# Two pairs of buffers for h's parts, and the first and last gate of each FFN in halves

## The reference

```python
def swiglu(x, w_gate, w_up, w_down):
    return (jax.nn.silu(x @ w_gate) * (x @ w_up)) @ w_down
...
        x = layer_norm(ALPHA * x + FFN_RESIDUAL * swiglu(x, ffn1_w_gate[l], ffn1_w_up[l], ffn1_w_down[l]),
                       ln1_g[l], ln1_b[l])
```

## Time and profile before

| | |
|---|---|
| median of 3 runs | 958.84 us (958.73 to 960.05) |
| the profiled execution's own time | 960.52 us |
| its span, first to last instruction | 958.5 us |
| mean granted TensorE clock | 0.998 |
| TensorE busy | 947.2 us, 99% of the span |
| VectorE busy | 853.7 us, 89% |
| ScalarE busy | 633.1 us, 66% |

### The profile page before, as it was taken

How to read it: one execution, slowest core, us unless ns; L and a number is a source line. 1 busy time by engine, 2 the same in 40 slices (tenths; PEclk the granted TensorE clock), 3 DMA queues, 4 the chain that set the end, 5 groups by cost and what they waited for, 6 DMA issues and landing times.

```text
span 958.5 us, 15322 instructions
## 1 busy us (share of the span) xinstructions
PE 947.2 (99%) x5418; PEld 817.6 (85%) x5418; DVE 853.7 (89%) x1119; ACT 633.1 (66%) x771; POOL 26.7 (3%) x55
## 2 busy tenths in 40 slices
PE   9999999999999999999999999999999999999996
PEld 9978888888788988888998888898888889888885
DVE  6999998966899999998999999988578989999986
ACT  6666665568884667675566767655688765667653
POOL 0000000001101000000000000000010100000000
PEclk9999999999999999999999999999999999999999
DMA  8576645672344565555636484654633445555554
GB/s 318 209 264 229 253 175 178 217 263 89 132 154 159 217 211 212 185 212 185 220 132 220 176 306 175 219 177 177 220 143 119 171 159 202 221 176 220 175 188 154
DMA packets 34653, 187.28 MB, mean 195 GB/s; under 512 B 3888, under 2 KB 3888, under 8 KB 19504
## 3 DMA queue, kind: packets, MB, share of 16 engines
q1 hardware_dynamic: 33120, 177.22, 51.4%
q0 software_dynamic: 1488, 9.45, 2.5%
HBM read 185.61 MB, written 1.05 MB: 195 GB/s over the span
## 4 chain that ended last, share of the span: by engine, by line
PE 91%; DVE 6%; issue 1%; DMA 1%; ACT 0%; DVEq 0%; POOL 0%; SPq 0%; ACTq 0%; POOLq 0%
PE bank L1599 67%; PE bank L1455 8%; PE bank L1457 8%; PE bank L1456 8%; PE bank L1518 1%; DVE w_lo L952 1%; DVE w_lo L909 1%; DMA raw<-stream 1%; DVE stick_t L931 1%; PE bank L1830 1%; DVE h_lo L1143 0%; DVE w_lo L959 0%; DVE stick_t L938 0%; DVE stick_t L941 0%; DVE w_lo L918 0%
## 5 line engine op out<-in xcount | busy, mean ns | idle before, releaser
L1599 PE MATMUL bank<-xT,w_hi 128*128 128x512 f32 (+1 forms) x1248 | 397.2, 387 | 0.0
L1599 PEld LDWEIGHTS bank<-xT,w_lo 128*128 128x128 f32 x1200 | 223.2, 188 | 49.7
L1599 PE MATMUL bank<-xT,w_lo 128*128 128x256 f32 x1200 | 234.6, 278 | 0.0
L510 ACT ACTIVATE w_hi<-raw 128x2048 fp32r<-128x2048 f32 x116 | 221.8, 1912 | 2.0 <-DMA raw<-stream 1.9
L1599 PEld LDWEIGHTS bank<-xT,w_hi 128*128 128x128 f32 x1248 | 198.0, 189 | 6.0 <-issue 0.9
L909 DVE TENSOR_TENSOR w_lo<-raw,w_hi 128x2048 fp32r<-128x2048 f32 x54 | 123.5, 2287 | 10.2 <-ACT w_hi L510 10.0
L651 ACT ACTIVATE ez<-bank 128x512 f32<-128x512 f32 x64 | 38.5, 601 | 104.0 <-PE bank L1599 104.0
L1599 PE MATMUL bank<-w_hi,h_hi 128*128 128x512 f32 x252 | 98.6, 391 | 2.3 <-DVE h_lo L1143 2.3
L1599 PE MATMUL bank<-w_lo,h_hi 128*128 128x512 f32 x252 | 98.6, 391 | 0.0
L1599 PE MATMUL bank<-w_hi,h_lo 128*128 128x512 f32 x252 | 98.4, 391 | 0.0
L1455 PE MATMUL bank<-xT,w_hi 128*128 128x256 f32 x304 | 86.2, 284 | 0.0
(11 more groups left out here) (189 smaller groups left out, 1577.7 us busy)
## 6 DMA issues: line engine op xcount, KB each, us to landing
raw<-stream SPq DMA_DIRECT2D x110, 1024.0 KB, 4.8
raw<-stream SPq DMA_DIRECT2D x110, 512.0 KB, 4.5
lnp<-ln_gb POOLq DMA_DIRECT2D x6, 1024.0 KB, 5.1
band<-rel_band POOLq DMA_DIRECT2D x2, 1024.0 KB, 9.8
xn<-x POOLq DMA_DIRECT2D x1, 1024.0 KB, 6.7
out<-xn SPq DMA_DIRECT2D x4, 256.0 KB, 2.0
qT<-first SPq DMA_DIRECT2D x2, 384.0 KB, 4.1
kT<-first SPq DMA_DIRECT2D x2, 384.0 KB, 5.1
```

Of the source, the lines that this page charges most:

```text
L510: nc.scalar.activation(w_hi[:, at(slot if into is None else into)], raw[:, slot, :], ACT.Copy).then_inc(hi_ready, 1)
L1599: return nc.tensor.matmul(o, w, x, start=start, stop=stop, skip_group_check=True)
```

## The change

Each pair of h_hi and h_lo gets a twin, in space that attention uses (sp_hi, sp_lo). Step j uses pair j mod 2, and so the loops over j on three engines are written with two steps in a body. With two pairs, high_h(j) need not wait for the products of unit j - 1; it moves ahead of copy_gate(j, 0) on ScalarE, and low_h(j) moves ahead of two subtractions on VectorE. gate(1) and gate(SF) become two halves like the other gates, with five matmuls between them; ScalarE copies both halves, and VectorE adds them. In the first FFN up of unit 1 goes to bank 7, not 6. Around the end of an FFN some of VectorE's instructions change places.

```diff
+        H_HI, H_LO = ((h, flat(s)[:, 0:7 * P].rearrange("p (i t) -> p i t", i=7))
+                      for h, s in ((h_hi, sp_hi), (h_lo, sp_lo)))
...
-                def high_h(j):
+                def high_h(j, k):
                     act.wait_ge(hsum_done, seven_step(l, f, j) + 1)
-                    nc.scalar.activation(h_hi[:, :, :], hs[:, 1:8, :], ACT.Copy).then_inc(hhi_done, 1)
+                    nc.scalar.activation(H_HI[k][:, :, :], hs[:, 1:8, :], ACT.Copy).then_inc(hhi_done, 1)
...
-                def last_of_h_and_parts(j):
+                def last_parts(j):
                     act.wait_ge(unit_used, used(l, base + 3 * j + 1))
-                    high_h(j)
                     split_last_parts_hi(l, f, j)
 
-                def step(j, more=True):
+                def step(j, k, more=True):
                     up_hi(j + 1)
+                    high_h(j, k)
+                    copy_gate(j, 0)
                     differences(j)
-                    copy_gate(j, 0)
-                    last_of_h_and_parts(j)
+                    last_parts(j)
                     copy_gate(j, 1)
...
-                differences(1)
-                up_hi(2)
-                last_of_h_and_parts(1)
-                act.wait_ge(hf_done, it(l, f, 1) + 1)
-                silu(2, 5)
-                next_gate(1)
-                copy_up(2, 0)
-                next_pure(2)
-                copy_up(2, 1)
-                with act.Fori(2, SF - 1) as j:
-                    step(j)
-                step(SF - 1, more=False)
+                step(1, 1)
+                with act.Fori(1, (SF - 1) // 2) as i:
+                    for k in range(2):
+                        step(2 * i + k, k)
+                step(SF - 1, 0, more=False)
                 split_hi(l, base + 3 * SF + 3, 0, first[0] + 1 + SF)
+                copy_gate(SF, 0)
...
-                silu(FP - 1, 3 * SF + 2)
+                copy_gate(SF, 1)
                 split_hi(l, base + 3 * SF + 5, 2, first[2] + 1 + SF)
+                silu_sums(SF)
...
-                def low_parts(j):
+                def low_parts(j, k):
                     split_up_lo(l, base + 3 * j + 3, 0)
+                    low_h(j, k)
+                    split_up_lo(l, base + 3 * j + 3, 1)
                     split_differences_lo(l, f, j)
-                    split_up_lo(l, base + 3 * j + 3, 1)
-                    low_h(j)
                     split_last_parts_lo(l, base + 3 * j + 4)
                     gate_sum(j)
...
+                split_lo(l, base + 3 * SF + 3, 0)
                 gather(l, f, 2)
-                split_lo(l, base + 3 * SF + 3, 0)
...
                 gather(l, f, 3)
+                gate_sum(SF)
                 split_lo(l, base + 3 * SF + 4, 1)
                 split_lo(l, base + 3 * SF + 5, 2)
                 last = 2 * l + f == 2 * DEPTH - 1
+                gated(FP - 1, 3 * SF + 3, M[1])
                 if not last:
                     dve.wait_ge(next_first_hi, 2 * l + f + 1)
...
-                gate(1)
-                step(1, first=True)
-                with pe.Fori(2, SF - 1) as j:
-                    step_with_gate(j)
-                step_with_gate(SF - 1, stop=True)
-                rest(stop=True)
-
-                gate(SF)
+                gate_half(1, 0)
+                rest(0, start=True)
+                gate_half(1, 1)
+                step(1, 1)
+                with pe.Fori(1, (SF - 1) // 2) as i:
+                    for k in range(2):
+                        step_with_gate(2 * i + k, k)
+                step_with_gate(SF - 1, 0, stop=True)
+                gate_half(SF, 0)
+                rest(0, stop=True)
+                gate_half(SF, 1)
```

More of the change, by code:

```diff
@@ L611, in ffn @@
                                              ACT.Copy).then_inc((first_hi, hi_ready)[half], 1)
-                    high_h(0)
+                    high_h(0, 0)
                     first_unit_hi()
@@ L1165, in ffn @@
                     split_pure_lo(l, f, 0)
-                    low_h(0)
+                    low_h(0, 0)
                     split_differences_lo(l, f, 0)
@@ L1184, in ffn @@
                     if j == 0 and r < 0:
-                        gated(j + 1, 3 * j + 3, bank[6])
+                        gated(j + 1, 3 * j + 3, bank[7])
                         split_lo(l, base + 3 * j + 5, 2)
@@ L1193, in ffn @@
                     split_pure_lo(l, f, j + 1)
[L1194 to L1203, removed]
                 def gate_sum(j):
@@ L1225, in next_unit @@
                     h_sums(j + 1)
-                split_last_parts_lo(l, base + 7)
+                low_parts(1, 1)
                 next_unit(1)
[L1229 to L1233, removed]
+                with dve.Fori(1, (SF - 1) // 2) as i:
+                    for k in range(2):
+                        low_parts(2 * i + k, k)
+                        next_unit(2 * i + k)
+                low_parts(SF - 1, 0)
                 split_lo(l, base + 3 * SF + 2, 2)
@@ L1253, in ffn @@
                     nc.vector.tensor_tensor(w_lo[:, c], raw[:, 0, HALVES[0]], w_hi[:, c].bitcast(F32), ALU.subtract)
-                gated(FP - 1, 3 * SF + 3, M[1])
+                dve.wait_ge(hhi_done, it(l, f, FP - 1) + 1)
+                nc.vector.tensor_tensor(hl_lo[:, :, :].rearrange("p c (b t) -> p c b t", b=2), h_pair,
+                                        hl_hi[:, :, :].bitcast(F32).rearrange("p c (b t) -> p c b t", b=2),
+                                        ALU.subtract).then_inc(hlo_done, 1)
                 if not last:
@@ L1619, in ffn @@
                 base = FFN_BASE[f]
-                def gate(j):
-                    pe.wait_ge(silu_done, it(l, f, j) + 1)
-                    pe.wait_ge(up_copied, 2 * wide(l, f, j) + 2)
-                    columns(l, base + 3 * j + 2, 2, bank[0])
                 def gate_half(j, c):
@@ L1646, in up_half, with product @@
                     wide_half(bank[0], 0, c).then_inc(unit_used if c else up_first, 1)
-                def product(m, start=False, signal=None, parts=(0, 1, 2)):
+                def product(k, m, start=False, signal=None, parts=(0, 1, 2)):
                     a, b = WINOGRAD[m]
                     w = at(1, seven(b))
-                    h = (h_hi[:, a, :], h_hi[:, a, :], h_lo[:, a, :])
+                    h = (H_HI[k][:, a, :], H_HI[k][:, a, :], H_LO[k][:, a, :])
                     d = (w_hi[:, w], w_lo[:, w], w_hi[:, w])
@@ L1658, in product, with rest, step @@
                         last.then_inc(signal, 1)
-                def rest(stop=False):
-                    product(6, signal=m_done if stop else None, parts=(1, 2))
-                    product(4, signal=unit_used)
-                def step(j, stop=False, first=False):
+                def rest(k, start=False, stop=False):
+                    product(k, 6, signal=m_done if stop else None, parts=(1, 2))
+                    if start:
+                        pe.wait_ge(hf_done, it(l, f, 1) + 1)
+                    product(k, 4, start, unit_used)
+                def step(j, k, stop=False):
                     n = seven_step(l, f, j)
```

67 lines of the change are left out of this document (30 added, 37 removed).

## The result

The change made the kernel slower by a little: median 962.09 us over 11 runs (961.45 to 962.35) against 959.36 of the kernel before (11 runs, 958.62 to 960.05). The ratio is 1.0028, 95% interval 1.0020 to 1.0036. The forecast was 958.2 us with a range to 960.4, so both the sign and the range were wrong. The profiled execution of the change took 962.09 us with a span of 960.3 us, against 960.52 and 958.5 before. So the two traces show 1.8 us of the 2.7 between the medians, since the profiled execution of before lay above its median.

What follows compares the result with a forecast made beforehand. It took TensorE, busy 947.2 of 958.5 us, as the bound. Terms +0.16 + 2 x 0.02 - 0.24 - 0.76 gave -0.80, or -0.54 without the late load; between them, 958.84 - 0.67 = 958.2 us, range 955.6 to 960.4.

Steps and rivals of the forecast that it cites:

- The end of an FFN: Last gate of each FFN: halves save 0.19 us, what follows the gated product is unchanged; 0.76 us in all.
- The gated product's margin: End of the second FFN: VectorE free at 466.71, gated product may start at 466.73, so it just fits, by 0.02 us.
- The waits at the first gates: Before gate_half(j, 1), TensorE waits for ScalarE's copy behind high_h: 0.67 and 1.10 us in the first FFN, 0.11 in the second and third.
- VectorE's delay of 0.40: First FFN, unit 2: gate_sum(1) takes 0.60 where a 0.20 wait stood, so h_sums(2) ends 0.40 us later.
- the 2.86 that the new buffers were to bring: Two waits of TensorE for h_lo, 1.52 and 1.14 us, go, with twice 0.10 of restart.
- three signs of being wrong: h_sums(2) moves by more than 0.4, the gated product starts later than 0.3 after the columns, or span falls over 2 us.
- The late load: Fourth FFN: a weight load landed late, perhaps in that execution alone; without it the sum is -0.54 us, not -0.80.
- Gates in halves: First and last gate of each FFN: two halves take 5.56 us against 5.75, 0.19 less for each of eight gates, 1.52.
- VectorE becomes the bound: Slower rival: eight more sums on VectorE, 4.8 us, all on the path, less 1.52 saved; 962.1 us, 9%.
- The waits just go: Faster rival: the gate's copy isn't held by high_h, gain 4.4 us, 954.5; needs h_sums(2) 1.1 us sooner; 8%.
- The double bodies: Slower rival: two-step loop bodies miss their code at backward branches, 8.5 us where engines overlap, 966.7 us; 3%.

Runs made afterwards that it cites:

- last_whole: The changed kernel with the last gate by columns() and no gate_sum there, VectorE's new order at the end kept; 961.37 us, ratio 1.0021.
- tail_before: The changed kernel with the whole end of an FFN as in the kernel before: last gate by columns(), no sum, VectorE's old order; 959.52 us, ratio 1.0002.
- tail_order: The changed kernel with the first half split back ahead of the gated product and the other ahead of hl_lo, gate still in halves; 962.32 us, ratio 1.0029.
- copy_first: The changed kernel with ScalarE's copy of the gate's first half ahead of high_h in every step; 958.53 us, ratio 0.9991.
- after_again: The changed kernel, unedited, run and profiled a second time; 962.81 us, ratio 1.0028 to the kernel before.
- before_again: The kernel before the change, unedited, run and profiled a second time; 959.72 us, ratio 0.9997.
- after_pad: The changed kernel with 64 unused semaphore increments at the head of TensorE's program, shifting its code; 971.19 us, ratio 1.0123.
- copy_buffers: The changed kernel with the gate's copy ahead of high_h, the old FFN end, and the first gate by columns() too; 957.25 us, ratio 0.9975.
- copy_tail_before: The changed kernel with the gate's copy ahead of high_h and the old FFN end, first gate still in halves; 956.25 us, ratio 0.9966.
- pool_half: The changed kernel with the first half split of the next stage's low weights at an FFN's end given to GpSimd; 962.27 us, ratio 1.0027.

## Why the prediction was wrong

**The end of an FFN is the step that failed.** The prediction said: "What follows is the same in both: one half of a split (1.22) between gated and hl_lo, only another half. So 0.19 in each FFN, 0.76 in all." That counts the instructions between the gated product and hl_lo alone, and there it is right. But the half split that was ahead of the gated product had to go somewhere, and it went behind hl_lo, ahead of the layer norm. The distance from the gated product to the norm's first addition grew by 1.24 us, and TensorE waited 0.64, 0.99 and 0.80. last_whole against tail_before shows that the order alone costs 1.85 us. tail_order shows that putting it back ahead of the gated product doesn't mend it, as long as gate_sum(9) is there. Undoing the whole end wins 2.6 us (tail_before), 0.78 of them in the second FFN's late load, in place of the 0.76 that it was to bring.

**The gated product's margin held.** It starts 0.30 after the columns (175.22 after 174.92), as worked out. The margin, 0.02 in the forecast, was 0.11 (in the second FFN VectorE's last split ends at 468.49, and the product starts at 468.60). But I worked it out for the change's order and didn't ask what had been moved out to make it fit.

**The waits at the first gates.** The mechanism was right: no wait for h_lo, one for soft_t at the places named. The first was 0.66, forecast 0.67. The second was 1.41, forecast 1.10: the term mis-sized was VectorE's delay of 0.40. h_sums(2) ended 0.99 later than before. Of that 0.27 was there before unit 1 began, 0.40 is gate_sum(1) as forecast, and the other 0.32 came at L1122, which waited 0.56 here and hardly before. It waits as long in every trace of a kernel whose first gate is in halves, copy_first and after_again among them; why is open. copy_first shows what this holding of the copy costs in all: 3.56 us, more than the 2.86 that the new buffers were to bring. Of the prediction's three signs of being wrong this was the one that showed: h_sums(2) moved by 0.99, not 0.4; the gated product wasn't late, and the span didn't fall.

**The late load.** "The late load may belong to that execution alone" was wrong. before_again has it again, and after_again has the change's one. It moved from the fourth FFN to the second: the fourth won 1.5 us where 0.43 was forecast, the second lost 0.98 where 0.11 was forecast. I had taken the load as fixed in the fourth and absent elsewhere. after_pad shows that moving TensorE's code takes the second FFN's away. That the fetch delays the load rests on these two loads in all twelve traces: 6.2 to 6.7 in seven cases with a fetch, 4.6 to 5.8 in seventeen without. How it does so is not shown, and it isn't the only thing that can: other loads took over 6.5 us without a fetch.

**Gates in halves** gave TensorE the 0.19 us each that was forecast, and the kernel kept it where VectorE had room (copy_buffers against copy_tail_before). At the end of an FFN it had none.

**The rivals.** "VectorE becomes the bound" ended nearest, and that its 962.1 is the measured time is luck: it is the price of eight sums on the path, which no trace shows. The point that it named as deciding, when VectorE reaches the gated product, was not the one either: it was what VectorE did after it. It was right in the engine, and 9% was little for an engine with a margin of 0.02 us. "The waits just go" needed an earlier h_sums(2); copy_first removed these waits without one, by the order of ScalarE's list, though with 958.53 and not 954.5. The double bodies cost nothing: in the change's loop from 366 to 450 us, with two backward branches of each of three engines, no transfer of q8 and one small one of q14 is listed, and step times are 15.9 us as before. (tail_before has one of q8 and one of q14 in the same stretch.) The Trainium skill (Runtime: NRT & Kernel Launch, section on instruction fetch) speaks of a fetch at a taken branch out of the window held; these rows don't show one at each branch, and no run here shows whether a body of this loop goes out of that window:

```profile
q1 hardware_dynamic: 3163, 16.76, 54.6%
q14 instruction: 1, 0.01, 0.0%
```

## What to carry to other kernels

When an instruction is moved to make room at one place, follow it to the place where it now stands and ask who is next in line there: the price of this change was half a split that left the way of one consumer and stood in the way of the next. A new pair of buffers frees two orders, not one: the early write is only worth having if it isn't put ahead of something that the critical engine waits for sooner. And where a forecast finds a margin of hundredths of a microsecond on an engine, what that engine does ahead of it and behind it deserves a sum of its own, not a rival at 9%.

## What the runs showed of the hardware

A weight load of 1 MB usually takes 4.8 us here (the median on the page). Two such loads took 6.2 to 6.7 us in the seven cases in which a transfer of the instruction queue fell into them, and 4.6 to 5.8 in the seventeen in which none did; 64 more instructions on TensorE were enough to move the transfer out of one of them. Whoever adds instructions to one engine may in this way move a stall in another.

64 semaphore increments on TensorE ahead of its first matmul took 9.29 to 10.64 us, 0.145 to 0.166 each.

VectorE and GpSimd, both at subtractions from SBUF to SBUF, slowed each other (pool_half): GpSimd's 128x1024 subtraction took 3.95 us in place of the 2.40 at 292.74, and VectorE's 128x512 subtraction 1.32 in place of 0.69. The gated product, which VectorE ran in GpSimd's stretch as well and which reads PSUM, kept its 0.69.
